# Value pass of a sparse-attention layer: prompt work of each step moved from between three value tiles to in front of them

## The chip, the cores and the metric

The kernel runs on one NeuronCore of a Trainium2 chip. The metric is the device time of one execution in microseconds (us); smaller is better. The time of the kernel before is 3293.39 us, the median of three runs (3290.66, 3293.39 and 3293.66).

## The reference

The reference is one inference step of a small decoder trunk for two groups at once: a prompt of 256 tokens, and 8 sample sequences with one new token each and 2048 past tokens. It has a state-space layer, then a native-sparse-attention layer, each followed by a feed-forward block. Only the attention matters here:

```python
def nsa_mixer(hn, pos, kv, w_q, w_gate, b_gate, w_o):
    q = rope((hn @ w_q).reshape(bsz, t, N_HEADS, HEAD_DIM), pos)     # 16 heads of 128, 4 KV heads
    gates = jax.nn.sigmoid(hn @ w_gate + b_gate)...
    o_cmp, p_grp = cmp_branch(q, pos, kv['k_cmp'], kv['v_cmp'])      # compressed keys
    idx, ok = select_blocks(p_grp, pos, kv['n_slc'])
    o_slc = kv['slc_fn'](q, pos, idx, ok)                            # selected blocks
    o_win = kv['win_fn'](q, pos)                                     # window of 512
    o = gates[:, :, 0] * o_cmp + gates[:, :, 1] * o_slc + gates[:, :, 2] * o_win
    return o.reshape(bsz, t, N_HEADS * HEAD_DIM) @ w_o
```

Each branch is `softmax(q k * scale + mask) v`. Everything is float32.

## The kernel before

All projections are matmuls of a float32 weight split into two parts; they fill most of the time and keep TensorE (PE) busy. Between the query projection and the output projection stands the attention. It streams 164 tiles of 128 x 1024 float32 (512 KB each) of the samples' cached keys and values through a ring of 7 buffers (`AHEAD`, array `TILE`): first the 80 key tiles, then in the *value pass* the 84 value tiles, v = 0 to 83 (16 of the window, 64 of the selected blocks, 4 compressed). The load of tile v + 7 starts when tile v was used (`att_used`, line 1942): SyncE (SP) issues one half of each selected tile and ScalarE (ACT) the other (line 2532).

PE uses a value tile in `values_pe` (line 2361): eight matmuls in which the stationary operand has four columns, so that the four KV heads' matmuls stand in four column groups of the array. The trace shows them as 16 records of L2370.

The prompt's attention is done beside these tiles. It has 24 *items*, k = 0 to 23: half qt of the prompt (128 tokens) x KV head g x branch br, br fastest. An item of branch 0 has 15 keys; one of branch 1 or 2 has 128 keys in the first half (k below 12) and 256 in the second (k from 12 on). A *step* is three tiles, v = 3k, 3k+1 and 3k+2 (`divmod(v, 3)`), and an item goes through these stations, one after the other:

- *scores*, PE, L2194, from `prompt_scores_pe`. It waits until the first operation of the mask of item k - 1 has read PSUM (`sc_used`).
- *mask*, VectorE (DVE), L2234, L2236, L2239: mask, row maximum, its negative. In `beside_values_dve` at v = 3k+1.
- *exp*, ACT, L2276, four pairs of instructions. In `beside_values_act` at v = 3k+2.
- *probs*, DVE, (L2250, L2252,) L2254 to L2261. At v = 3(k+1).
- *turn*, PE, L2208: transposes. At step k + 2. It also waits for the take of item k - 1 (`pt_taken`).
- *take*, ACT, L2285: copies the turned rows to SBUF. At v = 3(k+2)+2, just before the exp of item k + 2.
- *outputs*, PE, L2220, at step k + 3; three items (one o) add up in one PSUM bank. The first of them waits until the bank was read (`po_used`).
- *copy*, DVE, L2267, `prompt_out_dve`, once for each o.

Each engine works through its own list strictly in the order that the code issues it; engines meet only at semaphores. What sets the order is therefore these lines:

- PE: `attention_pe` calls `beside_values_pe(pe, v)` and then `values_pe` for each tile. Before the change the scores stand in front of tile 3k, the turn in front of 3k+1, the outputs in front of 3k+2.
- ACT: `attention_act` calls `beside_values_act(act, v)` and then, for v = 9 to 72, `load_tile(..., (1,))`, which waits until tile v was used. So ACT comes to the take and exp at v = 3k+2 only after tile 3k+1 was used by PE.
- DVE: `beside_values_dve(dve, v)`, with no wait for tiles.

In the first steps (v = 6 to 16) PE also turns the samples' probabilities (L2430, L2435, L2446) and waits for their copies. After the last tile ACT and DVE copy the accumulated values, PE transposes them, and the output projection begins; SP issues its weight loads (L374) as soon as tiles 81, 82 and 83 were used.

Of the kernel before, what the change touches and what calls it, by code (L numbers as in the profile page):

```python
# [109 lines left out]
def trunk_kernel(nc, io, out):  # L110
# [2053 lines left out]
    ITEMS = [(qt, g, br) for qt in range(2) for g in range(G) for br in range(3)]  # L2164
# [5 lines left out]
    def keys_of(item):  # L2170
        qt, g, br = item
        return NCMPP if br == 0 else P * (qt + 1)

    def score_view(k):

        n = keys_of(ITEMS[k])
        if n <= P:
            return PSUM[:, SCORE_BANK + k % 2, :].rearrange("p (r n) -> p r n", r=HREP)[:, :, 0:n]
        return PSUM[:, SCORE_BANK:SCORE_BANK + 2, :].rearrange("p b (r n) -> p (b r) n", r=2)[:, :, 0:n]

    def prompt_rows(k):
        return SP2[:, k % 3, :, :] if k % 3 < 2 else SP2X[:, :, :]

    def prompt_scores_pe(pe, k):
        qt, g, br = item = ITEMS[k]
        if k == 0:
            pc_dve.wait(pe, "k rows")
            pc_act.wait(pe, "v rows")
            pe.wait_ge(rope_done, len(ROPED))
        else:  # L2190
            pe.wait_ge(sc_used, k)
        for r in range(HREP):
            keys = KCP[:, g * NCMPP:(g + 1) * NCMPP] if br == 0 else KVT[:, 2 * br, g, 0:keys_of(item)]
            last = nc.tensor.matmul(score_view(k)[:, r, :], QT[:, HREP * g + r, qt * P:(qt + 1) * P], keys, start=True, stop=True)  # L2194
        last.then_inc(sc_done, 1)

    def parts_of(k):

        n = keys_of(ITEMS[k])
        return [(kc, min(P, n - kc * P)) for kc in range(-(-n // P))]  # L2200

    def prompt_turn_pe(pe, k):
        pe.wait_ge(pr_done, k + 1)
        if k >= 1:
            pe.wait_ge(pt_taken, k)
        for kc, w in parts_of(k):
            for r in range(HREP):
                last = nc.tensor.transpose(PSUM[0:w, PROBS_BANK + kc, r * P:(r + 1) * P], prompt_rows(k)[:, r, kc * P:kc * P + w], IDENT[:, :])  # L2208
        last.then_inc(pt_done, 1)

    def prompt_outputs_pe(pe, k):
        qt, g, br = ITEMS[k]
        parts = parts_of(k)
        pe.wait_ge(pt_taken, k + 1)
        o = k // 3
        if br == 0 and o >= 1:
            pe.wait_ge(po_used, o)
        for kc, w in parts:
            v = VCP[0:w, g, :] if br == 0 else VNAT[0:w, br - 1, kc, g * DH:(g + 1) * DH]
            last = nc.tensor.matmul(PSUM[:, OUT_BANK, :], v, PTP[0:w, k % 2, kc, :], start=br == 0 and kc == 0,  # L2220
                                    stop=br == 2 and kc == len(parts) - 1)
        last.then_inc(pv_done, 1)
# [40 lines left out]
    def prompt_out_dve(dve, o):  # L2263

        qt, g, _ = ITEMS[3 * o]
        dve.wait_ge(pv_done, 3 * o + 3)
        V.tensor_copy(QT[:, HREP * g:HREP * g + 4, qt * P:(qt + 1) * P], PSUM[:, OUT_BANK, :].rearrange("p (r t) -> p r t", r=4)).then_inc(po_used, 1)  # L2267
# [37 lines left out]
    def link_dve(dve, ins):  # L2305

        chain[0] += 1
        ins.then_inc(ch_dve, 1)
        dve.wait_ge(ch_dve, chain[0])
# [108 lines left out]
    def beside_values_pe(pe, v):  # L2418

        k, stage = divmod(v, 3)  # L2420
        if stage == 0 and k < len(ITEMS):
            prompt_scores_pe(pe, k)
        if stage == 1 and 2 <= k <= len(ITEMS) + 1:
            prompt_turn_pe(pe, k - 2)
        if stage == 2 and 3 <= k <= len(ITEMS) + 2:
            prompt_outputs_pe(pe, k - 3)
        if v == 6:
            sp_dve.wait(pe, "new probs")
            for k in range(2):
                last = nc.tensor.transpose(PSUM[0:32, SPARE_BANK, k * P:(k + 1) * P], RTW[:, k, :], IDENT[:, :])  # L2430
            sp_pe.made_by(last, "new turned")
        if v == 7:
            sp_dve.wait(pe, "new kept")
            for k in range(2):
                last = nc.tensor.matmul(PSUM[:, SPARE_BANK, 2 * P:3 * P], SNAT[:, 3 + 2 * k, :], RTK[0:32, k, :], start=k == 0, stop=k == 1)  # L2435
            sp_pe.made_by(last, "new values")
        if v in (9, 11, 13, 15):
            q = (v - 9) // 2
            if q == 0:
                sp_dve.wait(pe, "new added")  # L2440
            elif q % 2:
                sp_act.wait(pe, f"slc kept {q - 1}")
            else:
                sp_dve.wait(pe, f"slc kept {q - 1}")
            for j in range(4):
                last = nc.tensor.transpose(PSUM[:, SPARE_BANK, j * P:(j + 1) * P], S2[:, (4 * q + j) * P:(4 * q + j + 1) * P], IDENT[:, :])  # L2446
            sp_pe.made_by(last, f"slc turned {q}")
# [89 lines left out]
    def take_group_dve(dve, m):  # L2537

        dve.wait_ge(ks_done, 2 * TS * (m + 1))
        src = PSUM[:, 4 + m % 2, 0:2 * P]  # L2540
        if m < WIN_GROUPS:
            lo = 1 if m == 0 else 0
            link_dve(dve, V.tensor_copy(S2W[:, 2 * P * m + lo:2 * P * (m + 1)], src[:, lo:2 * P]))
            V.tensor_reduce(DM[:, 26 + m:27 + m], S2W[:, 2 * P * m + lo:2 * P * (m + 1)], AX.X, ALU.max).then_inc(sc_taken, 1)
            return
        j = m - WIN_GROUPS
        s = S2[:, 2 * P * j:2 * P * (j + 1)]
        link_dve(dve, V.tensor_tensor(s.rearrange("p (b k) -> p b k", k=64), src.rearrange("p (b k) -> p b k", k=64),
                                      BLK[:, 4 * j:4 * j + 4].unsqueeze(2).to_broadcast([P, 4, 64]), ALU.add))
        V.tensor_reduce(DM[:, 32 + j:33 + j], s, AX.X, ALU.max).then_inc(sc_taken, 1)  # L2550

    def negmax_dve(dve, name, parts, new, at):

        link_dve(dve, V.tensor_reduce(DM[:, at:at + 1], parts, AX.X, ALU.max))
        link_dve(dve, V.tensor_tensor(DM[:, at:at + 1], DM[:, at:at + 1], new, ALU.max))
        sp_dve.made_by(V.tensor_scalar(DM[:, at + 1:at + 2], DM[:, at:at + 1], -SCALE, None, ALU.mult), name + " negmax")
# [78 lines left out]
    def beside_values_dve(dve, v):  # L2635
        k, stage = divmod(v, 3)
        link = lambda ins: link_dve(dve, ins)
        if v == 0:
            take_group_dve(dve, GROUPS - 1)
            dve.wait_ge(sc_taken, GROUPS)  # L2640
            negmax_dve(dve, "slc", DM[:, 32:40], DM[:, 20:21], 4)
        if v == 3:
            sp_act.wait(dve, "slc new exp")
            link(V.tensor_reduce(DM[:, 6:7], DM[:, 12:16], AX.X, ALU.add))
            factor_dve(dve, 0, DM[:, 6:7])
            for q in range(4):
                last = V.tensor_scalar(S2[:, 512 * q:512 * q + 512], S2[:, 512 * q:512 * q + 512], DM[:, 7:8], None, ALU.mult)
            sp_dve.made_by(last, "slc probs")
            V.tensor_scalar(RTW[:, 0, :], BD[:, :], DM[:, 24:25], None, ALU.mult)
            sp_dve.made_by(V.tensor_scalar(RTW[:, 1, :], BD[:, :], DM[:, 25:26], None, ALU.mult), "new probs")  # L2650
        if stage == 0 and k >= 6 and k % 3 == 0:
            prompt_out_dve(dve, k // 3 - 2)
        if stage == 0 and 1 <= k <= len(ITEMS):
            prompt_probs_dve(dve, k - 1)
        if stage == 1 and k < len(ITEMS):
            prompt_mask_dve(dve, k)
        if v == 7:
            sp_pe.wait(dve, "new turned")
            sp_dve.made_by(V.tensor_copy(RTK[0:32, :, :].rearrange("p k c -> p (k c)"), PSUM[0:32, SPARE_BANK, 0:2 * P]), "new kept")
        if v == 8:  # L2660
            sp_pe.wait(dve, "new values")
            sp_dve.made_by(V.tensor_copy(NEWV[:, :], PSUM[:, SPARE_BANK, 2 * P:3 * P]), "new added")
        if v in (12, 16):
            q = (v - 10) // 2
            sp_pe.wait(dve, f"slc turned {q}")
            sp_dve.made_by(V.tensor_copy(SCT[:, 4 * q:4 * q + 4, :].rearrange("p j c -> p (j c)"), PSUM[:, SPARE_BANK, :]), f"slc kept {q}")
# [329 lines left out]
```

## Time and profile before

| | |
|---|---|
| median of three runs | 3293.39 us |
| the profiled execution | 3290.76 us, of which the span that the profile shows is 3288.9 us |
| PE busy | 3206.5 us, 97% of the span |
| DVE busy | 2032.2 us, 62% |
| ACT busy | 1553.7 us, 47% |
| the value pass | about 2149 to 2296 us of the span |

The page gives the span in 40 slices of 82 us, as busy tenths of each engine; the value pass lies in the 27th and 28th:

```profile
PE   7999999999999999999999999999999999999998
PEld 6899889889999999999999997855999999999998
DVE  7999988865655544555665546455665554455566
ACT  4555555644544444444554433344554444444454
PEclk9999999999999999999999999989999999999999
```

A busy PE row says little here, since matmuls overlap and waits of a fraction of a microsecond vanish in a slice. What counts is who waits for whom inside the value pass, which other views show.

### The profile page before, as it was taken

To read this page: it belongs to the slowest core of one execution; us is meant where nothing else is said; L and a number is where in the kernel's file an instruction comes from. 1 tells how busy PE (TensorE), PEld (TensorE's weight loads), DVE (VectorE), ACT (ScalarE), POOL (GpSimd) and SP (SyncE) were. 2 spreads that over 40 slices of the span, in tenths; PEclk is the share of its full clock that TensorE was granted. 3 is DMA by queue.
4 is the path that set the end of the run, shared out by engine and by line. 5 is a ranking of instruction groups with operands and counts; after the bars stand their busy time and mean duration, and the time that the engine had idled before them with its cause. 6 is when DMAs were issued, how large, how long until landed. Compare 5 with 4: busy or idle time off the path is not lost.

```text
span 3288.9 us, 69206 instructions
## 1 busy us (share of the span) xinstructions
PE 3206.5 (97%) x27708; PEld 3055.5 (93%) x27708; DVE 2032.2 (62%) x2281; ACT 1553.7 (47%) x1927; POOL 539.2 (16%) x477
## 2 busy tenths in 40 slices
PE   7999999999999999999999999999999999999998
PEld 6899889889999999999999997855999999999998
DVE  7999988865655544555665546455665554455566
ACT  4555555644544444444554433344554444444454
POOL 5666566620000000000000006000000000000000
PEclk9999999999999999999999999989999999999999
DMA  6445544456556555655556659889565655665553
GB/s 179 143 147 156 166 145 147 145 164 180 173 179 183 181 186 178 184 171 193 173 179 193 185 187 296 286 287 288 176 190 173 191 181 184 177 185 181 183 173 133
DMA packets 384392, 608.42 MB, mean 185 GB/s; under 512 B 52537, under 2 KB 144986, under 8 KB 383882
## 3 DMA queue, kind: packets, MB, share of 16 engines
q1 hardware_dynamic: 351738, 539.06, 52.7%
q10 hardware_dynamic: 29392, 60.86, 5.4%
q0 software_dynamic: 3024, 5.22, 0.4%
q8 instruction: 162, 2.65, 0.3%
q14 instruction: 76, 0.62, 0.1%
HBM read 594.83 MB, written 26.94 MB: 189 GB/s over the span
## 4 chain that ended last, share of the span: by engine, by line
PE 78%; DVE 14%; POOL 2%; issue 2%; ACT 2%; DMA 1%; SPq 0%; ACTq 0%; DVEq 0%; POOLq 0%
PE psum L407 22%; PE psum L408 22%; PE psum L409 22%; DVE rows_rest L1344 2%; PE psum L2322 2%; DVE turned L1403 2%; POOL prod_pool L1557 2%; PE psum L2332 1%; PE psum L1023 1%; PE psum L2370 1%; DVE normed_chunk L1428 1%; DVE turned L1394 1%; DVE state_ri L1411 1%; PE psum L1044 1%; PE psum L2220 1%
## 5 line engine op out<-in xcount | busy, mean ns | idle before, releaser
L390 DVE TENSOR_TENSOR w_rest<-w_raw,w_head 128x1024 fp32r<-128x1024 f32 x776 | 973.2, 1266 | 950.5 <-ACT w_head L386 949.7
L386 ACT ACTIVATE w_head<-w_raw 128x1024 fp32r<-128x1024 f32 x776 | 907.2, 1182 | 943.9 <-PE psum L409 906.4
L407 PE MATMUL psum<-act_head,w_head 128*128 128x264 f32 x4224 | 1204.5, 285 | 7.0 <-DVE act_rest L2757 5.8
L408 PE MATMUL psum<-act_rest,w_head 128*128 128x264 f32 x4224 | 1201.5, 284 | 0.0
L409 PE MATMUL psum<-act_head,w_rest 128*128 128x264 f32 x4224 | 1201.4, 284 | 0.0
L407 PEld LDWEIGHTS psum<-act_head,w_head 128*128 128x128 f32 x4224 | 824.5, 195 | 7.9 <-issue 6.0
L408 PEld LDWEIGHTS psum<-act_rest,w_head 128*128 128x128 f32 x4224 | 825.1, 195 | 0.2
L409 PEld LDWEIGHTS psum<-act_head,w_rest 128*128 128x128 f32 x4224 | 824.6, 195 | 0.0
L407 PE MATMUL psum<-hid_head,w_head 128*128 128x264 f32 x1408 | 400.0, 284 | 0.0
L408 PE MATMUL psum<-hid_rest,w_head 128*128 128x264 f32 x1408 | 399.9, 284 | 0.0
L409 PE MATMUL psum<-hid_head,w_rest 128*128 128x264 f32 x1408 | 399.9, 284 | 0.0
L1744 POOL TENSOR_TENSOR hid_rest<-prod_val,hid_head 128x1056 f32 x22 | 54.4, 2471 | 1748.0 <-ACT hid_head L1711 1748.0
L1044 PE MATMUL psum<-rows_head,w_head 128*128 128x256 f32 x1024 | 302.4, 295 | 2.1 <-DVE rows_rest L1344 1.4
L1046 PE MATMUL psum<-rows_head,w_rest 128*128 128x256 f32 x1024 | 291.2, 284 | 0.0
L1045 PE MATMUL psum<-rows_rest,w_head 128*128 128x256 f32 x1024 | 290.6, 284 | 0.0
L408 PEld LDWEIGHTS psum<-hid_rest,w_head 128*128 128x128 f32 x1408 | 274.4, 195 | 0.0
L409 PEld LDWEIGHTS psum<-hid_head,w_rest 128*128 128x128 f32 x1408 | 274.4, 195 | 0.0
L407 PEld LDWEIGHTS psum<-hid_head,w_head 128*128 128x128 f32 x1408 | 274.2, 195 | 0.0
L1178 ACT ACTIVATE rows_head<-psum 128x512 fp32r<-128x512 f32 x256 | 140.3, 596 | 213.5 <-PE psum L1023 213.5
L1044 PEld LDWEIGHTS psum<-rows_head,w_head 128*128 128x128 f32 x1024 | 195.3, 191 | 15.1 <-issue 14.6
L1045 PEld LDWEIGHTS psum<-rows_rest,w_head 128*128 128x128 f32 x1024 | 195.8, 191 | 0.0
L1046 PEld LDWEIGHTS psum<-rows_head,w_rest 128*128 128x128 f32 x1024 | 194.9, 190 | 0.0
(421 smaller groups left out, 4092.3 us busy)
## 6 DMA issues: line engine op xcount, KB each, us to landing
w_raw<-in_ffn_w_gate SPq DMA_DIRECT2D x176, 512.0 KB, 4.3
w_raw<-in_ffn_w_up SPq DMA_DIRECT2D x176, 512.0 KB, 4.4
w_raw<-in_ffn_w_down SPq DMA_DIRECT2D x176, 512.0 KB, 3.7
w_raw<-in_cache_cmp_k SPq DMA_DIRECT2D x256, 128.0 KB, 2.6
w_raw<-in_cache_cmp_v SPq DMA_DIRECT2D x256, 128.0 KB, 2.6
w_raw<-in_ssm_w_glu SPq DMA_DIRECT2D x64, 512.0 KB, 4.1
w_raw<-in_ple_w_gate SPq DMA_DIRECT2D x64, 512.0 KB, 4.3
w_raw<-in_kv_w SPq DMA_DIRECT2D x48, 512.0 KB, 3.7
```

Of the source, the lines that this page charges most:

```text
L386: nc.scalar.activation(pairs(WH, u), tiles_of(RAW, u), ACT.Copy).then_inc(head_done, 1)
L390: nc.vector.tensor_tensor(pairs(WL, u), tiles_of(RAW, u), pairs(WH, u).bitcast(F32), ALU.subtract).then_inc(rest_done, 1)
L407: nc.tensor.matmul(o, wh, head, start=k == 0, stop=False)
L408: nc.tensor.matmul(o, wh, rest, start=False, stop=False)
L409: last = nc.tensor.matmul(o, wl, head, start=False, stop=k == UK * kunits - 1)
L1044: nc.tensor.matmul(o, WH[:, part, w], hi, start=t == 0, stop=False)
L1045: nc.tensor.matmul(o, WH[:, part, w], lo, start=False, stop=False)
L1046: last = nc.tensor.matmul(o, WL[:, part, w], hi, start=False, stop=t == TAPS - 1)
L1178: nc.scalar.activation(head_rows(k, m // 2, m % 2), page_rows(n), ACT.Copy).then_inc(cmp_head, 1)
L1344: nc.vector.tensor_tensor(rest_rows(k, m // 2, m % 2), page_rows(n), head_rows(k, m // 2, m % 2).bitcast(F32), ALU.subtract).then_inc(cmp_ ...
L1403: last = nc.vector.tensor_tensor_scan(GB[:, t, h, :], m, GB[:, t, h, :], 0.0, ALU.mult, ALU.add)
L1557: nc.gpsimd.tensor_tensor(M12[:, :, :, :], states_in(p), sines(p, 0), ALU.mult).then_inc(pool_rot, 1)
```

## The change

In front of tile 3k PE now issues the scores of item k, the turn of item k - 2 and the outputs of item k - 3, and then the three tiles 3k, 3k+1 and 3k+2 with no prompt work between them. On DVE the copy of output o moves from the start of v = 9o+18 (ahead of the probs there) to the end of v = 9o+17. ACT is not touched.

```diff
     def beside_values_pe(pe, v):
 
         k, stage = divmod(v, 3)
-        if stage == 0 and k < len(ITEMS):
-            prompt_scores_pe(pe, k)
-        if stage == 1 and 2 <= k <= len(ITEMS) + 1:
-            prompt_turn_pe(pe, k - 2)
-        if stage == 2 and 3 <= k <= len(ITEMS) + 2:
-            prompt_outputs_pe(pe, k - 3)
+        if stage == 0:
+            if k < len(ITEMS):
+                prompt_scores_pe(pe, k)
+            if 2 <= k <= len(ITEMS) + 1:
+                prompt_turn_pe(pe, k - 2)
+            if 3 <= k <= len(ITEMS) + 2:
+                prompt_outputs_pe(pe, k - 3)
         if v == 6:
@@ beside_values_dve
-        if stage == 0 and k >= 6 and k % 3 == 0:
-            prompt_out_dve(dve, k // 3 - 2)
+        if stage == 2 and k >= 5 and k % 3 == 2:
+            prompt_out_dve(dve, k // 3 - 1)
         if stage == 0 and 1 <= k <= len(ITEMS):
             prompt_probs_dve(dve, k - 1)
         if stage == 1 and k < len(ITEMS):
```

## Rows read from the trace of the kernel before

**Rows 1.** Busy time by stretch: window, length, PE, PEld, DVE, ACT, POOL, PEclk, DMA share, GB/s.

```profile
2164.00:2180.00 16.00, 16.00 (x134) 10.02 (x134) 5.33 (x18) 3.08 (x14) 0.00 (x0) 0.51 0.57 165
2192.00:2218.40 26.40, 26.40 (x385) 15.89 (x375) 15.33 (x49) 12.35 (x54) 0.00 (x0) 1.00 1.02 359
2253.00:2270.30 17.30, 17.30 (x206) 10.44 (x198) 10.80 (x24) 7.86 (x28) 0.00 (x0) 1.00 0.90 284
```

**Rows 2.** Waits, 2149 to 2298 us: who, for whom, us in total, times, longest.

```profile
ACT probs_t_p L2285 <- PE psum L2370: 55.3, 19, 7.2
...
PE psum L2370 <- DMA tiles<-cmp_v_scratch: 0.3, 1, 0.3
```

**Rows 3.** Timeline of PE, second half: start, us, engine, line, operation [idle before].

```profile
2235.81 2.00 PE L2194 MATMUL psum<-kv_t,q_t 128*128 128x256 f32 x8 [0.79 <-DVE scores_p L2234]
2237.73 0.62 PE L2370 MATMUL psum<-tiles,scores_st 128*4 128x128 f32 x16
2238.28 1.09 PE L2208 MATMUL psum<-ident,scores_p 128*128 128x128 f32 x8
2239.30 0.62 PE L2370 MATMUL psum<-tiles,scores_st 128*4 128x128 f32 x16
2239.85 1.99 PE L2220 MATMUL psum<-probs_t_p,v_rows 128*128 128x512 f32 x4
...
2253.06 2.00 PE L2194 MATMUL psum<-kv_t,q_t 128*128 128x256 f32 x8
```

**Rows 4.** The chain that ended last, in order of time: start, us, what.

```profile
2193.90 1.09 PE psum L2194 x8
2194.99 0.55 PE psum L2370 x16
2195.54 0.59 PE psum L2208 x4
...
2196.67 1.05 PE psum L2220 x2
...
2206.90 1.09 PE psum L2194 x8
...
2290.47 1.42 PE psum L2370 x48
2291.89 1.91 PE psum L2220 x4
...
2295.33 4.72 DMA w_raw<-in_nsa_w_o
```

**Rows 5.** Timeline of ACT: a take of the early steps; take and exp's start, second half.

```profile
2181.75 0.60 ACT L2285 ACTIVATE probs_t_p<-psum 128x512 f32<-128x512 f32 x1 [7.21 <-PE psum L2370]
...
2240.59 1.02 ACT L2285 ACTIVATE probs_t_p<-psum 128x1024 f32<-128x1024 f32 x1 [3.08 <-PE psum L2370]
2241.51 0.50 ACT L2276 ACTIVATE scores_p<-scores_p,soft_small 128x256 f32<-128x256 f32 x1
```

**Rows 6.** Timeline of DVE, second half: mask of item 15, mask, probs of 16, mask of 17.

```profile
2235.54 0.21 DVE L2234 TENSOR_TENSOR scores_p<-psum,cmpvis 128x60 f32<-128x60 f32 x1
...
2238.80 1.22 DVE L2234 TENSOR_TENSOR scores_p<-psum,causal 128x1024 f32<-128x1024 f32 x1
...
2243.61 0.17 DVE L2254 TENSOR_SCALAR soft_small<-soft_small 128x4 f32<-128x4 f32 x1 [2.14 <-ACT scores_p L2276]
...
2245.37 1.22 DVE L2234 TENSOR_TENSOR scores_p<-psum,causal 128x1024 f32<-128x1024 f32 x1
```

**Rows 7.** Timelines, first half: exp's start of item 10 (ACT), its mask and probs, next mask.

```profile
2210.96 0.40 ACT L2276 ACTIVATE scores_p<-scores_p,soft_small 128x128 f32<-128x128 f32 x1
...
2209.31 0.69 DVE L2234 TENSOR_TENSOR scores_p<-psum,causal 128x512 f32<-128x512 f32 x1 [0.23 <-PE psum L2208]
...
2212.64 0.17 DVE L2254 TENSOR_SCALAR soft_small<-soft_small 128x4 f32<-128x4 f32 x1 [1.72 <-ACT scores_p L2276]
...
2213.87 0.68 DVE L2234 TENSOR_TENSOR scores_p<-psum,causal 128x512 f32<-128x512 f32 x1
```

**Rows 8.** Timeline of PE: scores of item 2 at the start, turn of item 23.

```profile
2157.63 2.08 PE L2194 MATMUL psum<-kv_t,q_t 128*128 128x128 f32 x8 [4.17 <-DVE scores_p L2234]
...
2286.91 1.09 PE L2208 MATMUL psum<-ident,scores_p 128*128 128x128 f32 x8
```

## The prediction

> **What bounds the kernel now.** I read the page first: PE is busy nearly everywhere, and the change touches only the value pass, some 147 us or 4.5% of the span. So the question is what sets the pace of that pass, and by how little.
>
> The sums by stretch [rows 1] show the two regular parts, the first half of the prompt (128 keys) and the second (256 keys): PE is busy all the time in both, DVE and ACT at about 60% and 45%, and the DMA share is 1.02 and 0.90. The list of waits [rows 2] says that DMA is still not the bound: PE waited for a tile once, 0.3 us, at the very end. (A share near one means that loads are always queued, which seven buffers allow.) The timeline of PE [rows 3] shows the cadence: from the scores of item 16 to those of item 19, three steps, are 2253.06 - 2235.81 = 17.25 us. In the first half the same three steps are 2206.90 - 2193.90 = 13.00 us [rows 4]. PE stands without gaps in nearly all of it.
>
> But a second chain runs beside it almost as slowly. DVE does mask(k), waits for exp(k) on ACT, does probs(k), then mask(k+1). From mask(16) to mask(17) are 2245.37 - 2238.80 = 6.57 us, from mask(15), a 15-key item, to mask(16) 3.26 us [rows 6]. Three items cost 3.26 + 2 x 6.57 = 16.40 us against PE's 17.25. In the first half mask(10) to mask(11) is 4.56 us [rows 7], and three items cost 3.26 + 2 x 4.56 = 12.38 us against 13.00. So even if PE became free, no more than 0.85 us in each three steps of the second half and 0.62 us in the first could be won. The row of the scores of item 16 already carries 0.79 us of idle time that a DVE mask ended [rows 3].
>
> And the two chains are tied by ACT. ACT waits 55.3 us in 19 pieces for value tiles before it does a take [rows 2]: it must issue its half of the loads of tiles 3k and 3k+1 first, and each waits for the tile's use. That wait ends right before take and exp.
>
> **The change part by part.**
>
> *Fewer switches on PE (gain).* A tile alone takes 0.55 us until the next instruction, three tiles in a row 1.42 [rows 4]. Putting them together saves 3 x 0.55 - 1.42 = 0.23 us in each step. The switch from other work *to* a tile also disappears twice a step (scores go to turn and turn to outputs directly). The trace before doesn't show such a direct switch at full clock, so I bound it. Scores of 256 columns take 1.92 us (2237.73 - 2235.81) and of 128 columns 1.09; doubling adds 0.83 and leaves 0.26 that doesn't scale. A turn of eight takes 1.02, one of four 0.59, which leaves 0.16 [rows 3, 4]. The direct switches can save up to these 0.4 us a step, or nothing if they cost the same. I take 0.2, near twice the 0.11 by which a single tile exceeds its neighbour in a row of three. On PE alone this makes 0.4 us a step.
>
> What the row shows is 0.11 us lost each time PE leaves the four column groups of a tile. The Trainium skill (TensorEngine Tiling (Array Packing), Key Properties) says that a change of tiling mode, unlike a change of tile, drains the engine. The row agrees with it in kind. By that rule alone the change removes four of six drains in each step and makes the kernel faster; this is the first rival below, worked out there from rows.
>
> *The take and exp come later (loss).* This is the part that decides. Before, ACT's gate, the use of tile 3k+1, stood behind scores, tile, turn, tile. Now the outputs stand in front of it too. For item 16, with the scores started at 2235.81: before, tile 49 starts at 2239.30 [rows 3], the take starts 1.29 us later (2240.59), and exp(16) 0.92 us after that, at 2241.51 [rows 5], just when its mask is done; the gate was free. After: scores 1.92, turn 1.02 [rows 3], outputs 1.91, one tile 0.44 (the middle of the 1.42 for three [rows 4]) = 5.29, then 1.29 + 0.92: exp(16) starts at 2243.31, or 2243.1 with 0.2 saved in switches. It is 1.6 us late, and DVE waits for it.
>
> From there a loop closes: exp(16), probs(16), mask(17), exp(17), probs(17), first operation of mask(18), scores(19) (they wait for that operation), turn(17), outputs(16), tile 57, tile 58, take(17), exp(19). Its length: exp to probs 2243.61 - 2241.51 = 2.10; probs to mask 1.76; mask to exp 2241.51 - 2238.80 = 2.71; again 2.10 and 1.76; 0.27 from mask(18) to scores(19) (2235.81 - 2235.54) [rows 3, 5, 6]; together 10.70. Then 5.29 on PE and 2.21 on ACT. Sum 18.20, less 0.2 is 18.0 us for three steps, against 17.25 now. Before, the same loop had 1.80 less (3.49 from the scores' start to that of the second tile in place of 5.29), 16.4 us, and did not bind. So exp(22) starts at 2243.1 + 2 x 18.0 = 2279.1. Then exp, probs, mask, exp (2.10 + 1.76 + 2.71 = 6.57), and 2.10 + 1.9 to the end of probs(23): turn(23) starts at 2289.7, against 2286.91 [rows 8]. That is +2.8 us if the pass is on time at item 15.
>
> *First half and start (nearly level).* In the first half the same loop is exp to probs 1.68, probs to mask 1.23, mask to probs 3.33, 1.23, 0.27 [rows 7], together 7.74; on PE 1.09 + 0.59 + 1.05 + 0.44 = 3.17 [rows 4]; on ACT 1.29 and 0.60 less 0.1 of overlap. Sum 12.7, or 12.5 with 0.2 saved, against 13.00: a gain of 0.3 to 0.6 in each three steps, about -1.0 us from item 6 to item 12. In the early steps the loss comes first: take(2) and exp(4) wait for tile 13 [rows 5], and now outputs(1) stand ahead of that tile: 1.05 us at full clock, twice that while PE has half of it (0.51 until 2180 [rows 1]). A copy of the samples' probabilities queues behind exp(4) on ACT, and PE waits for them. I take +1.3 (1.0 to 2.1). Lateness at item 15: +0.3 (-0.6 to +1.3).
>
> *The end.* From turn(23) to the load that the chain then follows, issued at 2295.33 [rows 4], are 8.42 us of PE work now. After, the same work stands there plus one tile in front of tile 82 and fewer switches. But the last tiles now come in a rush, six in a row, while each load still starts seven tiles earlier: tile 82's when tile 75 was used. With 4.72 us for a load of the same size [rows 4], it lands about when it's wanted; if four loads queue, 1.5 us late. I take +0.2 (0 to 1.5).
>
> *Nothing.* DVE's list is the same instruction for instruction: between the old place of the copy and the new one stands no other DVE work; its cost of 0.7 us lies beside exp. It waits for outputs that PE now makes two tiles sooner. The new wait is PE's at outputs(3o), which needs the copy of o - 1; by then scores and turn have passed, about 2 us, so 0 to 0.3 us, inside the loops above.
>
> Sum: 2.8 + 0.3 + 0.2 = +3.3 us. The profiled execution took 3290.76 us and would take 3294.1; it is 2.6 us below the median of the runs, which is noise of the same size as the effect. On the median: 3293.4 + 3.3 = **3296.7 us**.
>
> With every bound at its good end (0.4 saved in switches: first exp(16) and then each loop 0.2 earlier, 0.6 in all; -0.6 at item 15, nothing at the end) the sum is 2.2 - 0.6 = +1.6 us; with every bound at its bad end 2.8 + 0.6 + 1.3 + 1.5 = +6.2.
>
> **Rivals.**
>
> *The gate is not reached*, because ACT has slack that I misread, and PE's gain counts up to DVE's chain. Four switches at the 0.11 us that the row shows for one are 0.44 us a step, 1.3 in three; DVE's chain cuts that to 0.62 x 3 in the first half and 0.85 x 4 in the second, 5.3 us in all: 3288 us. For it: PE is the full row. Against: ACT's order is fixed in the code, and its waits name L2370 [rows 2, 5].
>
> *Slower clock at the start.* PE idles 4.17 us before scores(2) [rows 8], and its clock is at 1.2 GHz until about 2180 [rows 1]. The new order shifts work and puts small waits of PE in this stretch. Each further microsecond at 1.2 GHz costs half a microsecond of PE. On top of +3.3, 6.6 us more of it pass the bound of 0.2%; until item 6 (10 us more) it gives 3296.7 + 5 = 3301.7. For it: the stretch was long although PE was busy for 16.00 of its last 16 us. Against: the new order is denser there, which could as well shorten it.
>
> **How the numbers follow.** Forecast (+1.6 to +6.2 us, so 3295.0 to 3299.6) 0.66; gate not reached 0.17; slower clock 0.17. A measurement of this kernel can tell about 0.2%, 6.6 us, from no change. The forecast and its bounds lie within that, and so does the gate case's 5.3 us unless the slow stretch also gets shorter (0.04 faster); the clock case passes the bound for most of its chance, 0.15 slower; same 0.81. The range 3290.5 to 3302.0 holds the forecast with its bounds, the median's own scatter of 3 us, and the nearer half of each rival.
>
> **What would show it.** Right: three steps of the second half at about 18.0 us between scores; exp of items 16, 19 and 22 some 1.6 us behind the end of their mask, the others at once; PE idle before scores of items 15, 16, 18, 19, ended by DVE masks; the first half at about 12.5; DVE's chain, not PE, in the chain that ended last; turn(23) 3 us later. Wrong: three steps of the second half under 17.25 (the gate is not where I put it), tiles that PE waits for before the last four, or a granted clock of 0.5 beyond 2184 us.

## The result, and the profile after

The changed kernel takes 3308.71 us (median of five runs, 3306.33 to 3310.78), the kernel before 3293.39 us (five runs, 3286.87 to 3294.97). The ratio is 1.0051, with a 95% interval of 1.0036 to 1.0065: slower by 15.3 us, where I had forecast 3296.7 us, +3.3, and a range that ended at 3302.0. By the bound of 0.2% that I had set, this is the outcome *slower*, to which I had given 0.15.

The profiled execution of the changed kernel took 3310.78 us, with a span of 3308.9 us; that is 20.0 us over the one of before. It is the slowest of the five runs, and the other four were 0.9 to 4.5 us shorter, so what the trace puts on each part is a little more than in the median. I measure the value pass from the start of the first scores to the start of tile 83. It was 147.0 us before and is 165.8 us after: +18.8. The rest of the span is 1.2 us longer, which I take for scatter. So the loss lies where the change is.

The page already shows something that a sum of waits can't (busy tenths in 40 slices of 83 us; the value pass is in the 27th and 28th):

```profile
PE   7999999999999999999999999989999999999998
...
PEclk9999999999999999999999999978999999999999
```

PEclk reads 7 and 8 in these two slices where it read 8 and 9 before: TensorE's granted clock is lower in the pass. Split by stretch, the second half of it alternates (columns as in [rows 1]: window, length, PE, PEld, DVE, ACT, POOL, PEclk, DMA share and rate):

```profile
2239.80:2246.60 6.80, 6.80 (x57) 3.78 (x56) 2.81 (x10) 3.27 (x15) 0.00 (x0) 0.50 0.72 247
2246.60:2260.30 13.70, 12.41 (x144) 8.64 (x143) 8.03 (x15) 4.53 (x14) 0.00 (x0) 1.00 0.63 228
2260.30:2267.10 6.80, 6.80 (x56) 3.81 (x56) 2.77 (x10) 3.29 (x15) 0.00 (x0) 0.50 0.69 218
2267.10:2280.80 13.70, 12.30 (x143) 8.31 (x141) 8.05 (x15) 4.23 (x13) 0.00 (x0) 1.00 0.69 231
2280.80:2287.60 6.80, 6.75 (x55) 3.84 (x56) 2.25 (x7) 3.43 (x15) 0.00 (x0) 0.50 0.65 210
```

In each period of 20.5 us the clock is at 1.2 GHz for 6.8 us and at 2.4 GHz for the other 13.7. The kernel before had 1.00 in its regular loop [rows 1, third row], and its windows from 2218.4 to 2296 us show 1.00 as well.

The waits answer to [rows 2] (2149 to 2320 us; us in total, times, longest):

```profile
ACT probs_t_p L2285 <- PE psum L2370: 67.8, 19, 6.2
...
PE psum L2194 <- DVE scores_p L2234: 9.9, 7, 4.2
...
PE psum L2370 <- DMA tiles<-cmp_v_scratch: 0.8, 1, 0.8
```

ACT waits 12.5 us longer for tiles. PE waits seven times for DVE before it may write scores, 9.9 us, of which 4.2 are the wait at the start that was there before [rows 8]; the wait of 0.79 us that [rows 3] show was the only other one then. Loads are still not the bound.

One loop on PE, which answers to [rows 3] (start, us, engine, line, operation, idle before):

```profile
2243.87 3.36 PE L2194 MATMUL psum<-kv_t,q_t 128*128 128x256 f32 x8
2247.06 1.04 PE L2208 MATMUL psum<-ident,scores_p 128*128 128x128 f32 x8
2247.94 1.88 PE L2220 MATMUL psum<-probs_t_p,v_rows 128*128 128x512 f32 x4
2249.75 1.49 PE L2370 MATMUL psum<-tiles,scores_st 128*4 128x128 f32 x48
...
2257.90 1.06 PE L2194 MATMUL psum<-k_cmp_p,q_t 128*128 128x15 f32 x8 [1.13 <-DVE scores_p L2234]
...
2260.04 1.78 PE L2220 MATMUL psum<-probs_t_p,v_cmp_p 15*128 15x512 f32 x2 [0.16 <-DVE q_t L2267]
2261.75 2.74 PE L2370 MATMUL psum<-tiles,scores_st 128*4 128x128 f32 x48
2264.42 3.32 PE L2194 MATMUL psum<-kv_t,q_t 128*128 128x256 f32 x8
```

From the scores of item 16 (2243.87) to those of item 19 (2264.42) are 20.55 us, and 21.07 to those of item 22 (2285.49). Before they were 17.25; I had forecast 18.0. Two things stand in these rows. PE is idle for 1.13 us before the scores of item 18, ended by the DVE mask, as forecast. And the last outputs, three tiles and scores of a loop take far too long: scores 2247.06 - 2243.87 = 3.19 us instead of 1.83 at full clock, three tiles 2.67 instead of 1.42. That is the low clock.

DVE and ACT at the same place (they answer to [rows 5, 6]): end of the mask of item 16; on ACT take and exp(16), then the loads and the take of the next loop; on DVE probs(16) and the first operation of mask(18).

```profile
2249.78 0.17 DVE L2239 TENSOR_SCALAR soft_small<-soft_small 128x4 f32<-128x4 f32 x1
```

```profile
2251.86 1.02 ACT L2285 ACTIVATE probs_t_p<-psum 128x1024 f32<-128x1024 f32 x1 [5.93 <-PE psum L2370]
...
2252.78 0.50 ACT L2276 ACTIVATE scores_p<-scores_p,soft_small 128x256 f32<-128x256 f32 x1
...
2271.08 1.48 ACTq L1944 DMA_DIRECT2D tiles<-in_cache_slc_v  x2
2272.66 1.02 ACT L2285 ACTIVATE probs_t_p<-psum 128x1024 f32<-128x1024 f32 x1 [6.17 <-PE psum L2370]
```

```profile
2254.87 0.17 DVE L2254 TENSOR_SCALAR soft_small<-soft_small 128x4 f32<-128x4 f32 x1 [4.93 <-ACT scores_p L2276]
...
2263.20 0.21 DVE L2234 TENSOR_TENSOR scores_p<-psum,cmpvis 128x60 f32<-128x60 f32 x1
```

Exp(16) starts 2.83 us after its mask is done (2249.95); before, it started just when the mask was done. The gate is where the prediction put it. The exps of items 12, 15, 18 and 21 are late too, by 1.54, 1.33, 1.36 and 1.83 us, where I had said that the others would start at once. Those of 15, 18 and 21 are not on the loop: the mask of item 19, which needs exp(18) and probs(18) before it, was still done 3.12 us before exp(19).

Where the 18.8 us of the pass arise (start of scores k, measured from the first scores):

| item | before | after | late | added |
|---|---|---|---|---|
| 6 | 40.97 | 40.15 | -0.8 | |
| 9 | 53.97 | 56.52 | +2.6 | +3.4 |
| 12 | 66.97 | 69.92 | +3.0 | +0.4 |
| 15 | 81.65 | 86.78 | +5.1 | +2.2 |
| 23 | 128.26 | 141.87 | +13.6 | +8.5 |
| tile 83 | 146.97 | 165.76 | +18.8 | +5.2 |

### The profile page after: what moved, and what is told of

It reads as the page before. It is cut to its first block, busy times and chain, and to the rows that moved or that the text cites. A ratio compares the mean times of both kernels' runs of the same rounds, so it can differ in the third digit from the quotient of the medians.

```text
span 3308.9 us, 69206 instructions
## 1 busy us (share of the span) xinstructions
PE 3215.3 (97%) x27708; PEld 3066.4 (93%) x27708; DVE 2032.6 (61%) x2281; ACT 1554.2 (47%) x1927; POOL 540.8 (16%) x477
## 4 chain that ended last, share of the span: by engine, by line
PE 77%; DVE 14%; issue 3%; ACT 2%; POOL 2%; DMA 1%; ACTq 0%; SPq 0%; DVEq 0%; POOLq 0%
PE psum L407 22%; PE psum L408 21%; PE psum L409 21%; DVE rows_rest L1344 2%; PE psum L2322 2%; DVE turned L1403 2%; POOL prod_pool L1557 2%; PE psum L2332 1%; PE psum L1023 1%; DVE normed_chunk L1428 1%; PE psum L2370 1%; DVE turned L1394 1%; DVE state_ri L1411 1%; PE psum L1044 1%; PE psum L1046 1%
```

## Experiments

Two theories stood after the result, and a rival. *Gate*: the outputs in front of tile 3k + 1 delay ACT's take and exp, and a loop through DVE, ACT and PE closes at some 18 to 18.5 us. *Clock*: the gate makes PE idle in pieces of over 1 us, the granted clock falls, and that makes the loop 2 to 3 us longer still. The rival, *bunching*: three tiles with nothing between them are themselves the harm (loads, buffers), whatever ACT does.

Every ratio below is to the kernel before, measured beside it on the same chip, with its 95% interval. The *pass* is always that of one profiled execution. Where an edit starts from the changed kernel, the copy on DVE stays in its new place.

### One part alone: the turn

Only the turn moves to the front; the outputs stay in front of tile 3k + 2.

```diff
-        if stage == 1 and 2 <= k <= len(ITEMS) + 1:
+        if stage == 0 and 2 <= k <= len(ITEMS) + 1:
             prompt_turn_pe(pe, k - 2)
```

> Of the change only the turn stands in front of tile 3k, behind the scores; the outputs stay in front of tile 3k+2. Theory G+C (the outputs in front of tile 3k+1 hold back ACT's take and exp, DVE waits for the exp, PE idles, and TensorE's clock falls because of that): ACT's gate is where it was, so exp of items 16, 19 and 22 starts within 0.6 us of its mask's end, no stretch at 1.2 GHz after 2200 us, three steps of the second half near 17 us, time 0 to 4 us below before (3290 to 3293). Theory B (tiles standing together, without work between them, starve TensorE or its loads): half of the bunching is here (two tiles in a row), so several us slower than before.

Measured: 3289.90 us, ratio 0.9997 (0.9987 to 1.0006), pass 147.2 us. Three steps of the first half are 12.30 us (13.00 before). So the turn in front of both tiles does no harm. It is no gain in the time either. One expectation missed: the clock was at 1.2 GHz for 3.4 us from 2234.9, and exp(16) behind it started 1.11 us after its mask.

### One part alone: the outputs

```diff
-        if stage == 2 and 3 <= k <= len(ITEMS) + 2:
+        if stage == 0 and 3 <= k <= len(ITEMS) + 2:
             prompt_outputs_pe(pe, k - 3)
```

> Of the change only the outputs stand in front of tile 3k, behind the scores; the turn stays in front of tile 3k+1, so no more than two tiles stand in a row. Theory G+C: the same work as in the changed kernel stands in front of tile 3k+1, plus one switch, so exp of items 16 and 19 is 1.5 to 3 us late, stretches at 1.2 GHz come back in each three steps, and the time is that of the changed kernel within 3 us (3306 to 3312). Theory B: clearly faster than the changed kernel, near 3300.

Measured: 3313.31 us, ratio 1.0065 (1.0048 to 1.0081), pass 167.0 us. The outputs alone are all of the loss; whether they cost a little more than the whole change can't be told, since the intervals overlap. One wait is longer than in the changed kernel, where it was 0.16 us: the copy on DVE stands behind a mask, and with only the scores ahead of them the outputs come too soon for it (PE timeline):

```profile
2259.71 1.06 PE L2194 MATMUL psum<-k_cmp_p,q_t 128*128 128x15 f32 x8 [0.56 <-DVE scores_p L2234]
2261.85 2.04 PE L2220 MATMUL psum<-probs_t_p,v_cmp_p 15*128 15x512 f32 x2 [1.08 <-DVE q_t L2267]
```

These outputs took 1.97 us until the next instruction, against 1.02 at full clock: here too the clock fell in each loop.

### Taking the gate away

The changed kernel, but SP issues both halves of the selected value tiles, so that ACT has no wait for tiles between its prompt instructions.

```diff
             beside_values_act(act, v)
-            if halved(SV_ALL + v + AHEAD):
-                load_tile(act, SV_ALL + v + AHEAD, (1,))
@@ SP's loop over the tiles
-            if halved(t):
-                load_tile(sp, t, (0,))
-            elif not by_act(t):
+            if not by_act(t):
                 load_tile(sp, t)
```

> The changed kernel, but SP issues both halves of each selected value tile, so ACT waits for no tile before its take and exp. Theory G+C: nothing holds exp back, DVE's chain (16.4 us for three items of the second half, 12.4 in the first) is all that is left, no stretch at 1.2 GHz after 2200 us; 4 to 7 us faster than before (3286 to 3290). Theory B (tiles standing together): as slow as the changed kernel, since the three tiles in a row stay. A rival to both, SP as the only issuer being too slow: PE waits for tiles in the first half.

Measured: 3295.81 us, ratio 1.0009 (1.0000 to 1.0019). Twelve of the 15 us are back, with scores, turn, outputs and tiles in the order of the change. That refutes bunching as the main cause. In the second half exp starts 0.04 us after its mask every time, and there is no fall of the clock from item 12 to item 23. (Its profiled execution, 3289.67 us, lies 6 us under its median. The mean granted clock of the ten executions goes from 0.991 down to 0.986, so some of the others held more time at 1.2 GHz than this trace, with 0.989.) The expected gain over the kernel before didn't come. The falls in other executions may be a part of it; in this one another wait took over (waits, 2149 to 2310 us):

```profile
ACT probs_t_p L2285 <- PE psum L2208: 29.5, 19, 3.7
...
PE psum L2370 <- DMA tiles<-cmp_v_scratch: 3.6, 3, 2.5
PE psum L2370 <- DMA tiles<-in_cache_slc_v: 3.4, 5, 0.9
```

ACT now waits for the turn and no longer for tiles, and PE waits 7.0 us for loads where it waited 0.3 before [rows 2]. Here that is the next limit behind the gate.

### The gate alone, in the old order

The kernel before, with take and exp of each step from the third on one tile later on ACT (behind the use of tile 3k + 2). Nothing is bunched.

```diff
-        if stage == 2:
-            if 2 <= k <= len(ITEMS) + 1:
-                prompt_take_act(act, k - 2)
-            if k < len(ITEMS):
-                prompt_exp_act(act, k)
+        if stage == 0 and k >= 3:
+            if 2 <= k - 1 <= len(ITEMS) + 1:
+                prompt_take_act(act, k - 3)
+            if k - 1 < len(ITEMS):
+                prompt_exp_act(act, k - 1)
+        if stage == 2 and k < 2:
+            prompt_exp_act(act, k)
```

> The kernel before, PE's and DVE's order untouched; only ACT does take(k-2) and exp(k) one tile later (at v = 3k+3 in place of 3k+2), so its gate is the use of tile 3k+2. Theory G+C (what matters is when ACT's gate opens, not how PE's work is grouped): the gate now opens 5.95 us after the scores' start in the second half, about 1.0 us later than in the changed kernel (1.83 + 0.87 + 1.81 + 0.44 = 4.95 there); the loop through it is 10.70 + 8.16 = 18.9 us plus what the clock adds, stretches at 1.2 GHz come back in the second half, and the kernel is as slow as the changed one or slower: 3307 to 3320. Theory B (grouping itself costs): no more than 2 us slower than before, since no tiles stand together.

Measured: 3302.94 us, ratio 1.0047 (1.0028 to 1.0066). A late gate alone makes the kernel slower, in the order of before. The loop came out as forecast: scores 16 at 2243.42, scores 19 at 2262.28, 18.86 us (PE timeline).

```profile
2243.42 1.99 PE L2194 MATMUL psum<-kv_t,q_t 128*128 128x256 f32 x8
...
2256.71 1.06 PE L2194 MATMUL psum<-k_cmp_p,q_t 128*128 128x15 f32 x8 [0.68 <-DVE scores_p L2234]
...
2262.28 0.92 PE L2194 MATMUL psum<-kv_t,q_t 128*128 128x256 f32 x3 [0.78 <-DVE scores_p L2234]
```

But the median stayed under what I expected (two of the five runs, 3310.45 and 3314.04 us, did not), and in the profiled execution the clock did not fall in these loops. PE's idle time is about as long in total but lies in two pieces of 0.68 and 0.78 us. Before these loops it fell once in this half, for 3.4 us from 2238.3, after a gap of 1.16 us before the scores of item 15. Not all of the loss is the loop: 3.8 us were there at the scores of item 6 (44.8 us after the first scores, 41.0 before). PE waited 3.70 us for a copy of DVE at tile 16, and 1.23 in the kernel before.

### The clock alone: work in PE's idle time

The changed kernel, with five matmuls of the identity into an unused PSUM bank in front of the scores of items 12, 15, 18 and 21 (and at step 24). They add work and change no result; at full clock PE idles in these places anyway.

```diff
         if stage == 0:
+            if k in (12, 15, 18, 21, 24):
+                for _ in range(5):
+                    nc.tensor.matmul(PSUM[:, SPARE_BANK, 0:P], IDENT[:, :], IDENT[:, :], start=True, stop=True)
             if k < len(ITEMS):
```

> The changed kernel with five more matmuls (identity by identity, about 1 us of TensorE, into a bank that is free then) in front of the scores of items 12, 15, 18 and 21 and of the turn of item 22, where PE waits for DVE's mask in the changed kernel. They are work added. Theory C (the clock's fall is a cause of its own): the gaps of 1.1 to 1.9 us are filled, the stretches at 1.2 GHz in the second half vanish or get fewer, three steps fall from 20.5-21 us to 18-18.5, and the kernel is 5 to 10 us faster than the changed one although it does more (3299 to 3304). Theory G alone (the late exp costs all of it, the low clock is only seen beside it): the same as the changed kernel or slower, 3308 to 3310.

Measured: 3304.11 us, ratio 1.0035 (1.0022 to 1.0047), pass 156.6 us instead of 165.8. More work, and the pass of the profiled execution is 9.2 us shorter. The time shows it less clearly: from 1.0051 to 1.0035 are some 5 us, and the intervals overlap between 1.0036 and 1.0047. The mean granted clock of whole executions points the same way: it was 0.984 or 0.985 in all five of the changed kernel and 0.986 to 0.991 in all 24 of the three versions with filler. The second half runs at full clock but for one stretch of 3.4 us (PE timeline, the filler's records are L2424; then the sums of one loop):

```profile
2261.13 1.99 PE L2194 MATMUL psum<-kv_t,q_t 128*128 128x256 f32 x8 [0.91 <-DVE scores_p L2234]
...
2272.89 1.38 PE L2424 MATMUL psum<-ident 128*128 128x128 f32 x10
2274.11 1.05 PE L2194 MATMUL psum<-k_cmp_p,q_t 128*128 128x15 f32 x8
...
2279.67 1.99 PE L2194 MATMUL psum<-kv_t,q_t 128*128 128x256 f32 x8 [0.92 <-DVE scores_p L2234]
```

```profile
2261.10:2279.60 18.50, 17.31 (x208) 12.22 (x208) 10.79 (x24) 7.80 (x28) 0.00 (x0) 1.00 0.79 258
```

The loop is 2279.67 - 2261.13 = 18.54 us: the length that the gate gives without the clock. The same loop of the changed kernel took 21.07, so the clock's share of it is 2.5 us.

With two matmuls instead of five, 0.71 us in the records instead of 1.38:

> As the changed kernel with filler matmuls at five places in the second half, but two at each place in place of five: 0.43 us of the 1.13 us gap are filled, 0.7 us stay idle. In the traces so far a gap of 1.13 us and more in front of the scores was followed by a fall of the clock, gaps of 0.68 to 0.79 us were not. Theory C (the length of PE's gap in one piece makes the clock fall): no or few stretches at 1.2 GHz in the second half, three steps near 18.5 us (10.70 + 4.95 + 1.96 + 0.92), time as with five fillers, 3301 to 3305. If nearly all of the gap must be filled: the stretches stay and the time is 3306 to 3310.

Measured: 3303.03 us, ratio 1.0027 (1.0016 to 1.0037), pass 158.1 us. The time is as good, but one of the falls stayed: 6.8 us at 1.2 GHz from 2258.4, in a loop of 21.12 us, where the loop before it, from the scores of item 15 to those of item 18, was 18.25. It followed a gap of only 0.49 us, and a gap of 1.21 us earlier in the same pass was followed by none:

```profile
2237.60 1.06 PE L2194 MATMUL psum<-k_cmp_p,q_t 128*128 128x15 f32 x8 [1.21 <-DVE scores_p L2234]
...
2255.85 1.06 PE L2194 MATMUL psum<-k_cmp_p,q_t 128*128 128x15 f32 x8 [0.49 <-DVE scores_p L2234]
...
2262.28 3.41 PE L2194 MATMUL psum<-kv_t,q_t 128*128 128x256 f32 x8
```

So with a little work in the gaps this execution had one fall of 6.8 us in the second half, where the changed kernel had four, but the length of one gap doesn't decide it.

A third version has the five matmuls and eight more, ahead of a wait of PE at tile 16, to see whether the slow start is the clock too:

```diff
             if t == SV:
+                for _ in range(8):
+                    nc.tensor.matmul(PSUM[:, SCORE_BANK, 0:P], IDENT[:, :], IDENT[:, :], start=True, stop=True)
                 sp_dve.wait(pe, "slc kept 3")
```

> As the changed kernel with five filler matmuls in front of items 12, 15, 18, 21 and turn 22, and eight more (about 1.7 us) in front of PE's wait for the last copy of the samples' probabilities ahead of tile 16, where PE idles 1.77 us and after which the clock fell for 10.2 us in the changed kernel (6.8 us in the run with the first five). Theory C: the stretch at 1.2 GHz near 2190 us goes, and the kernel is 2 to 4 us faster than with the five alone (3300 to 3302). If idle time isn't what makes the clock fall there: the same as with the five alone, 3304.

Measured: 3300.04 us, ratio 1.0023 (1.0014 to 1.0033), pass 154.0 us. The fall at 2190 is gone, but another comes at 2203.7 (6.8 us). Behind it the clock is at 2.4 GHz until the end of the pass: scores 16 to 19 take 18.25 us (20.55 in the changed kernel), 19 to 22 take 18.54 (21.07). From scores 6 to scores 12 the three kernels take 29.7 us (this one), 29.7 (five matmuls) and 29.8 (changed kernel), against 26.0 before. So this filler moved the fall and saved nothing there. Of the 2.6 us that this pass is shorter than that of the five matmuls, 2.1 were there at the scores of item 5 (32.1 us after the first scores against 34.2), ahead of the new matmuls: they are not the cause, and two executions of the same code differ by that much here. What makes the clock fall in the first half stays open.

### Half of the pass at a time

```diff
+        together = k >= 12
         if stage == 0 and k < len(ITEMS):
             prompt_scores_pe(pe, k)
-        if stage == 1 and 2 <= k <= len(ITEMS) + 1:
+        if stage == (0 if together else 1) and 2 <= k <= len(ITEMS) + 1:
             prompt_turn_pe(pe, k - 2)
-        if stage == 2 and 3 <= k <= len(ITEMS) + 2:
+        if stage == (0 if together else 2) and 3 <= k <= len(ITEMS) + 2:
             prompt_outputs_pe(pe, k - 3)
```

> The change for items from 12 on only (256 keys); the order of before up to there. Theory G+C says that the loop through ACT binds only in the second half: three steps of it at 20.5 to 21 us with a stretch at 1.2 GHz in each, exp of items 16, 19, 22 2 to 3 us late; 11 to 15 us slower than before (3303 to 3308). If the start carries half of the loss: no more than 8 us slower.

Measured: 3303.03 us, ratio 1.0036 (1.0023 to 1.0048). From scores 12 to tile 83 its profiled pass takes 95.5 us, the changed kernel's 95.8, the one of before 80.0. The falls are the same, 10.2 us from 2236.0 and then 6.8 us from 2259.9, 2280.4 and 2300.9. (Its profiled execution, 3310.43 us, was its slowest, with a mean granted clock of 0.983. Four of the six took 3300.7 to 3303.2 us at 0.986 or 0.987, so they held less time at 1.2 GHz.)

With `together = k < 12` instead:

> The change for items below 12 only. Theory G+C: the start loses some 2 to 4 us (outputs in front of tile 13, a copy that comes late, a stretch at 1.2 GHz near 2190), the first half's regular part wins a part of it back, and DVE's slack in the second half hides 1 us more: 0 to 4 us slower than before (3292 to 3297).

Measured: 3296.49 us, ratio 1.0008 (0.9998 to 1.0018), pass 150.8 us, +3.8. The early part alone can't be told from no change in the time. Most of the loss is the second half.

### The gate one tile earlier

If the gate is the cause, ACT may do take and exp behind tile 3k instead of 3k + 1, which in the changed kernel follows the outputs directly. The changed kernel with:

```diff
-        if stage == 2:
+        if stage == (1 if k >= 6 else 2):
             if 2 <= k <= len(ITEMS) + 1:
                 prompt_take_act(act, k - 2)
```

> The changed kernel, with ACT's take and exp from item 6 on at v = 3k+1 in place of 3k+2: its gate is the use of tile 3k, and one of the two loads that queue in front of it goes behind. Theory G+C: the take starts 1.29 us after tile 3k's start in place of 0.44 + 1.96 us, 1.1 us sooner, the loop is 17.4 us, PE's gaps fall under 0.7 us, no stretch at 1.2 GHz after 2200 us; the start keeps its loss. 4 to 7 us slower than before (3296 to 3299), 10 us faster than the changed kernel.

Measured: 3298.11 us, ratio 1.0014 (1.0005 to 1.0024), pass 153.8 us. The loop came out at 2271.89 - 2254.18 = 17.71 and, before it, 17.42 us:

```profile
2254.18 1.06 PE L2194 MATMUL psum<-k_cmp_p,q_t 128*128 128x15 f32 x8 [0.33 <-DVE scores_p L2234]
...
2259.75 1.99 PE L2194 MATMUL psum<-kv_t,q_t 128*128 128x256 f32 x8 [0.91 <-DVE scores_p L2234]
```

Take and exp one tile earlier on ACT give back some 11 us of the 15. Two expectations missed: the gaps of PE in the second half were up to 0.92 us, and the clock was at 1.2 GHz three times after 2200 us, for some 3.4 us each, from 2210.4, 2223.9 and 2275.3. Its pass is still 6.8 us longer than before, 2.7 of them by the scores of item 12, the rest behind.

The same edit on the version in which only the turn was moved:

> Only the turn in front of tile 3k (outputs in front of 3k+2 as before), and ACT's take and exp from item 6 on at v = 3k+1. Theory G: exp never waits for a tile; DVE's chain (12.4 and 16.4 us) and the loads' rate are all that is left. 1 to 4 us faster than before (3288 to 3291), the same as with the turn alone or 1 us better. If ACT's second load, now behind the exp, comes too late: PE waits for tiles and nothing is won.

Measured: 3291.39 us, ratio 0.9993 (0.9984 to 1.0002). Its loop from item 18 to item 21 is close to DVE's chain:

```profile
2251.36:2267.93 16.57, 16.57 (x203) 10.83 (x199) 10.95 (x26) 8.06 (x27) 0.00 (x0) 1.00 0.89 297
```

16.57 us between the scores of items 18 and 21, PE busy for all of it, against DVE's 16.4. ACT's earlier gate isn't what makes this loop: with the turn alone it was 16.57 too, and 16.31 in the version in which SP issues all loads. The pass is 144.1 us, 2.8 less than before, and that is below what the measurement can tell. No version beats the kernel before by a difference that can be measured.

## Why the prediction was wrong, step by step

*Right: the gate, its place and its sign.* The outputs in front of tile 3k + 1 are the part that does the harm (1.0065 alone, the turn alone 0.9997). Exp starts late at items 16, 19 and 22, by 2.83, 3.1 and 2.35 us (I had said 1.6); PE idles before the scores of items 15, 18 and 21, ended by DVE masks (not of 16 and 19, as I had also said: there the low clock kept PE busy past the mask); PE doesn't wait for selected tiles. The chain that ended last is not DVE's alone, as I had said: in one loop it runs on PE from the outputs of item 12 (2239.52) to the tiles before the take (2251.29), 11.8 us of some 20.5, and on ACT and DVE for the rest. "Gate not reached", to which I gave 0.17, is refuted.

*Right: the switches, a little larger than taken.* Scores to turn took 1.83 us instead of 1.92, turn to outputs 0.87 instead of 1.02, outputs to tile 1.81 instead of 1.91, three tiles 1.42: PE's list of a step is 5.93 us, 0.57 less than 6.50 before. I took 0.4, with 0.63 as its bound. What a direct switch between two groups of full-width matmuls saves is 0.09 to 0.15 us here. In the changed kernel all of this became idle time of PE.

The Trainium skill (TensorEngine Tiling (Array Packing), Key Properties) says that a change of tiling mode drains the engine. The rows agree in kind: the saving appears just where a change of mode is gone. But the rule alone says nothing of who waits for a tile, and by it alone this change would have been faster.

*Mis-sized: the gate's delay on ACT (1.29 us).* I took the time from the tile's start to the take from a row of before, where the loads of tiles 3k and 3k + 1 are issued at different times. With the tiles in a row, ACT issues both back to back: of the tiles that start at 2270.26 the second starts 0.44 us later, at 2270.70, and the take at 2272.66, 1.96 us later (1.68 in the loop before). My sum of 18.20, less 0.34 for the larger savings (5.29 becomes 4.95 on PE) and plus 0.67, is 18.5: what the kernel with five matmuls shows (18.54). This step was short by 0.5 us a loop.

*Missed: the clock in the second half.* This is the step that failed: "Each further microsecond at 1.2 GHz" was priced for the start alone, and in the loop of 18.0 us PE's idle time was taken as free, with no term for the clock. In fact each loop of the profiled execution has 6.8 us at 1.2 GHz and takes 20.55 or 21.07 us. The sign that I had named, a granted clock of 0.5 beyond 2184 us, did come. Its price can be worked out from rows in the first loop. Scores(16) take 3.19 us instead of 1.83: 1.36. Outputs and tiles from 2260.04 end at 2264.42, though at full clock scores(19) could have started when the first operation of mask(18) was done, 2263.41 plus the 0.03 that it takes: 0.98. Together 2.34; 20.55 - 2.34 = 18.2, which is the loop with the take at 1.68. In the next loop the same sum is 1.33 + 1.24 and leaves 18.5. So gate and clock together account for the loop to within a tenth of a microsecond, and the filler shows it from the other side: remove the falls and 18.54 us is left. In these loops the copy on DVE is on the path as well: the outputs of items 12, 15 and 18 wait 0.16 us for it, within the 0 to 0.3 that I had allowed. The point is that a fall in a loop that DVE and ACT set costs even there, since PE's work behind the idle time is on the loop.

*Missed: where the second half begins.* I let the loop begin at item 16. Items 13 and 14 have 256 keys too. The kernel with the change only from item 12 on loses 0.9 us between items 12 and 15 (15.54 us against 14.69), before any low clock of that half; the changed kernel loses 2.2 there, with 3.4 us at 1.2 GHz from 2222.8.

*Wrong in size: start and first half (forecast -0.6 to +1.3 at item 15, found +5.1).* The named rival, a slower clock at the start, is what happened, but later than I put it: not until item 6 (there the changed kernel was 0.8 us ahead, which is within the 2 us by which such starts differ), but from 2188.6 to 2198.8, beginning inside PE's wait for a DVE copy at tile 16:

```profile
2188.92 1.89 PE L2370 MATMUL psum<-tiles,scores_st 128*4 128x128 f32 x32 [1.77 <-DVE scores_st L2667]
```

The regular part from item 9 to 12 was 13.40 us, where I said 12.5 and it was 13.00 before.

*Wrong in size: from item 15 to turn(23) (+2.8 forecast, +12.1 found).* Turn(23) starts 155.6 us after the first scores, 138.3 before. That is 17.3 us late, 5.1 of them from before item 15. The last 3.7 of the 12.1 came behind the scores of item 23: turn(22) found the take before it late by the gate, and the clock fell again (turn(22), three tiles, turn(23)):

```profile
2299.99 1.06 PE L2208 MATMUL psum<-ident,scores_p 128*128 128x128 f32 x8 [1.91 <-ACT probs_t_p L2285]
...
2303.33 2.74 PE L2370 MATMUL psum<-tiles,scores_st 128*4 128x128 f32 x48
2306.20 1.94 PE L2208 MATMUL psum<-ident,scores_p 128*128 128x128 f32 x8
```

*The end (+0.2 forecast, 0 to 1.5 as bounds; +1.5 found).* From turn(23) to tile 83 are 10.16 us, 8.63 before. The wait for a load that I had priced is 0.8 us, 0.3 before. Turn(23) itself took 1.74 us until the next instruction instead of 0.87, since the clock was still low.

*The sum.* The size of the gate was right within a few microseconds: with the falls of the second half removed (all but 3.4 us) the loss from item 12 to tile 83 is 85.8 - 80.0 = 5.8 us, and 5.2 in the third filler version, which has none; I had about 3. The falls add some 10 us to that in the profiled execution (95.8 - 85.8), and the first half another 3. In the ratios of whole runs the three fillers give back 5 to 9 of the 15 us. My forecast priced a mechanism and left out what it sets off.

What stays open: why the clock falls after one gap and not after another (below), and so why the first half lost 3.8 us between items 6 and 12. That the falls of the second half come from PE's idle time rests on the filler, which takes most of them away and changes nothing else but to add work; the falls at the start rest on no experiment that moved the time.

## What to carry to other kernels

When work is moved ahead of an instruction that another engine's list waits for, follow that engine's list to its next wait and close the loop; here one item's outputs, moved in front of two tiles, lengthened the loop from 17.25 to 18.5 us. Then ask what the new idle time of PE does to its clock: a gap that is free in the sum can cost more than the gap, and a few matmuls of no use in it help to tell the two apart. And put the gated work of the other engine as early as its data allow: that took back 11 of the 15 us here.

## What the runs showed of the hardware that I had not expected

In loops in which PE was over 90% busy (12.41 us of the 13.70 at full clock, all of the 6.80 at low clock) the granted clock still fell to 1.2 GHz for 6.8 us at a time. In the changed kernel the idle time before the scores of items 15, 18 and 21 was 1.87, 1.13 and 1.14 us, and the clock fell 2.1 to 2.4 us after each of them ended (PE timeline; the row of item 18 stands above):

```profile
2237.38 1.06 PE L2194 MATMUL psum<-k_cmp_p,q_t 128*128 128x15 f32 x8 [1.87 <-DVE scores_p L2234]
...
2278.71 1.06 PE L2194 MATMUL psum<-k_cmp_p,q_t 128*128 128x15 f32 x8 [1.14 <-DVE scores_p L2234]
```

With gaps of 0.68 and 0.78 us spread over the loop (late gate in the old order) it didn't fall in the loops. But there are rows on both sides. When only the turn was moved a gap of 1.00 us was followed at once by 3.4 us at 1.2 GHz:

```profile
2229.37 1.06 PE L2194 MATMUL psum<-k_cmp_p,q_t 128*128 128x15 f32 x8 [0.86 <-DVE scores_p L2234]
...
2234.94 3.66 PE L2194 MATMUL psum<-kv_t,q_t 128*128 128x256 f32 x8 [1.00 <-DVE scores_p L2234]
```

The same gap of 1.00 us in the version with ACT's earlier gate was followed by none; there the gap of 0.86 us of the first row was missing. And 1.77 us before tile 16 was followed by a fall in the changed kernel and by none in the two in which only the turn was moved. What tips it these runs don't show.

Filler of 0.71 us per loop (1.0027) and of 1.38 us (1.0035) can't be told apart in the time; the intervals overlap.

An ACT that issues two loads in a row starts the next activation 0.4 to 0.7 us later than one that issued them apart: 1.68 and 1.96 us after the tile's start against 1.29.
